# Walking the pairs of row tiles from the longest to the shortest in both attentions of a hybrid encoder

## The reference, cut to what matters

```python
def _fox_attend(q, k, v, c_q, c_k, pos_q, pos_k):          # forgetting attention, 4 heads
    s = jnp.einsum('bqhd,bkhd->bhqk', q, k) * HD_B ** -0.5
    s = s + (c_q[..., :, None] - c_k[..., None, :])        # sums of log forget values
    s = jnp.where(pos_k[None, :] <= pos_q[:, None], s, -jnp.inf)
    return softmax(s) @ v

def _dsa_attend(q, k, v, iq, ik, iw, cid_q, cid_k, k_top): # sparse attention, 4 heads, one K/V
    score = sum over 8 index heads of relu(iq . ik) * iw   # admissible keys only
    sel = top 256 keys of each row by score
    return softmax(q . k[sel]) @ v[sel]
```

## Time and profile before

| | |
|---|---|
| median of three runs | 2187.8 us (2182.45, 2187.8, 2193.98) |
| the profiled execution | 2186.85 us, its span 2185.2 us |
| mean granted clock of TensorE | 0.972 |
| busy: TensorE, VectorE, ScalarE, GpSimd | 1951.6, 1398.9, 734.6, 263.3 us |
| forget attention of layer 1, pairs and unit 8 | 692.4 to 846.8 us |
| sparse attention of layer 1 | 846.8 to about 966 us |
| forget attention of layer 2, pairs and unit 8 | 1776.0 to 1921.3 us |

### The profile page before, as it was taken

The page is one execution under the profiler, slowest core; times in us unless marked ns, Lnnn a source line. Parts: engine busy times, 40 slices in busy tenths (PEclk is TensorE's granted clock), DMA queues, the critical chain, the costliest instruction groups (busy, mean ns, idle before and its releaser), DMA issues. The chain is left out here.

```text
span 2185.2 us, 27310 instructions
## 1 busy us (share of the span) xinstructions
PE 1951.6 (89%) x9690; PEld 1091.6 (50%) x9690; DVE 1398.9 (64%) x2963; ACT 734.6 (34%) x1678; POOL 263.3 (12%) x362
## 2 busy tenths in 40 slices
PE   3999999989997777989969999999999977789997
PEld 2534456555444555654445344565554455556443
DVE  3268498889796773442232784989898968634422
ACT  2352134333112333543333522334331024344422
POOL 0000133232100000001100002233221000000011
PEclk9999999999998889999979999999999999999999
DMA  7201213121413002314351022221214130032242
GB/s 276 97 25 70 75 59 124 59 86 43 140 37 78 16 3 90 92 40 153 111 200 61 21 74 73 90 95 58 99 44 125 37 74 15 3 94 88 84 153 103
DMA packets 151272, 178.34 MB, mean 82 GB/s; under 512 B 71408, under 2 KB 106736, under 8 KB 150864
## 3 DMA queue, kind: packets, MB, share of 16 engines
q1 hardware_dynamic: 123072, 139.19, 20.3%
q10 hardware_dynamic: 28064, 37.38, 4.8%
HBM read 119.72 MB, written 66.69 MB: 85 GB/s over the span
## 5 line engine op out<-in xcount | busy, mean ns | idle before, releaser
L908 PE MATMUL ps<-wring,xnT_arena 128*128 128x512 f32 (+2 forms) x2304 | 920.6, 542 | 0.0
L908 PEld LDWEIGHTS ps<-wring,xnT_arena 128*128 128x128 f32 x2304 | 404.5, 192 | 354.0 <-issue 337.3
L1754 DVE TENSOR_SCALAR_CACHE_REDUCE arena<-arena,theta 32x1056 bf16<-32x1056 f32 x496 | 461.0, 979 | 2.3
L1391 ACT COPY arena<-ps 128x512 f32<-128x512 f32 (+3 forms) x144 | 75.4, 524 | 448.4 <-PE ps L908 414.8
L1269 PE MATMUL ps<-wring,xnT_arena 128*128 128x512 f32 x512 | 223.8, 595 | 0.0
L2028 DVE TENSOR_REDUCE mneg<-ps 128x1 f32<-128x192 f32 (+9 forms) x148 | 114.0, 770 | 120.7 <-PE ps L1201 118.6
L1269 PEld LDWEIGHTS ps<-wring,xnT_arena 128*128 128x128 f32 x512 | 96.4, 191 | 115.3 <-issue 115.3
L2196 POOL TENSOR_TENSOR arena<-arena 128x1024 f32<-128x1024 f32 (+1 forms) x16 | 35.4, 2215 | 757.9 <-DVE arena L1980 568.8
L1044 PEld LDWEIGHTS ps<-arena 128*128 128x128 f32 x488 | 69.6, 193 | 107.0 <-DVE arena L1861 78.5
L1044 PE MATMUL ps<-arena 128*128 128x128 f32 x488 | 80.4, 288 | 39.6 <-DVE arena L1861 39.4
L1199 PE MATMUL ps<-xnT_arena,arena 128*128 128x512 f32 (+4 forms) x240 | 97.1, 525 | 10.6 <-DVE xnT_arena L1356 9.1
(11 more groups left out here) (269 smaller groups left out, 2529.7 us busy)
## 6 DMA issues: line engine op xcount, KB each, us to landing
projected<-arena ACTq DMA_DIRECT2D x130, 256.0 KB, 2.0
arena<-residual SPq DMA_DIRECT2D x34, 512.0 KB, 5.1
wring<-in_w_in SPq DMA_DIRECT2D x16, 1024.0 KB, 7.8
o_bc<-projected SPq DMA_DIRECT2D x36, 384.0 KB, 3.7
wring<-in_w_in SPq DMA_DIRECT2D x6, 2048.0 KB, 8.8
wring<-in_w_out SPq DMA_DIRECT2D x8, 1024.0 KB, 6.4
residual<-arena SPq DMA_DIRECT2D x16, 512.0 KB, 2.7
out<-arena SPq DMA_DIRECT2D x16, 512.0 KB, 4.0
```

Of the source, the lines that this page charges most:

```text
L908: o = mm(bank(pbank(k), 0, w_), xnT[:, c, t * P:(t + 1) * P], w, start=(c == 0), stop=(c == CH - 1))
L1391: nc.scalar.copy(stage[s][:, 0:wide], bank(pbank(k), 0, wide)).then_inc(p_ev, 1)
L1754: V.tensor_scalar(cmp_out[0][r, (i % 2) * WMAX:(i % 2) * WMAX + uw[u]], score[u][r], th_, 0.0, op, ALU.add, accum_out=into[r, i:i + 1]).th ...
```

## The change

The four pairs are listed in the reverse order, in both attentions: (3, 7), (2, 6), (1, 5), (0, 4). The sample unit stays first and unit 8 last. All else follows from the list.

```diff
-        UNIT_GROUPS = [["s"]] + [[t, t + 4] for t in range(NT - 5)] + [[NT - 1]]
+        UNIT_GROUPS = [["s"]] + [[t, t + 4] for t in reversed(range(NT - 5))] + [[NT - 1]]
         AU = [(m, u) for m in ("fox", "dsa") for group in UNIT_GROUPS for u in group]
         AJ = [(m, u, h) for m in ("fox", "dsa") for group in UNIT_GROUPS for h in (range(H) if group != ["s"] else [0]) for u in group]
```

## The result

The changed kernel takes 2197.84 us (median of 17 runs, 2190.69 to 2201.89) against 2188.7 us for the kernel before on the same chips (17 runs, 2181.1 to 2201.64). The two medians lie 9.1 us apart; the ratio of the two sets of runs is 1.0031, 95% interval 1.0016 to 1.0047, which is 3.5 to 10.3 us slower with 6.8 in the middle, and inside the 0.5% that I had set as the bound of no difference. The forecast was 2194 us, with +7.2 us. So the sum was right; whether its terms were is another question. The profiled execution took 2200.29 us, its span 2198.6 at a mean granted clock of 0.971. That execution is 2.5 us above the median of its kernel.

What follows compares the result with a forecast made beforehand. VectorE was taken to bound all four forget pairs, TensorE the sparse attention. Per layer 1.6 + 3.0 - 1.0 = +3.6, twice, +7.2 us on 2186.85: forecast 2194 us, range 2172 to 2208.

Steps and rivals of the forecast that it cites:

- no difference: Whole kernel: a rival with 2187 to 2189 us, chance 0.12; differences within 0.5% (11 us) count as none.
- Start: Before the first forget pair: eight key tiles turned instead of five, five load buffers, first score 3.0 us later per layer.
- The pairs' order: Forget pairs: TensorE bounds the first, VectorE the others; 117.0 us against a mean of 115.4, +1.6 per layer.
- The three tiles: Inside the forget pairs: three key-tile turns disappear, worth between 0 and 5.3 us, taken as -1.0 per layer.
- Unit 8 of the forget attention: After the forget pairs: its work stays; between -6.3 in one layer and +6.3 in the other, taken as 0.
- The sparse attention: Sparse pairs: TensorE bounds, so order does not matter; 1.9 us of idle time may hide or show, taken as 0.
- The chances: Whole kernel: same within 0.5% 0.52, slower 0.30, faster 0.18.
- Slower by the clock: Rival, first pair and unit 8 of the forget attention: TensorE's clock drops, giving 2205 us; chance 0.30.
- Faster by stalls: Rival, forget attention: pair 0+4's turn-back never late, tiles worth 5.3 us, unit 8 31.32 us in both layers; 2173 us, chance 0.18.

Runs made afterwards that it cites:

- e4: The change itself run again, both attentions reversed, against the kernel before: 2195.8 us, ratio 1.0037.
- e1: Pairs reversed in the forget attention only, sparse attention in the old order, against the kernel before: 2190.02 us, ratio 1.0009.
- e2: Pairs reversed in the sparse attention only, forget attention in the old order, against the kernel before: 2193.89 us, ratio 1.0021.
- e11: The kernel before without its last two search rounds and with penalties set to zero, key tiles still inside the pairs: forget pairs 85.40 and 85.38 us.
- e7: The change without the last two search rounds and with penalties set to zero: 2136.26 us in one run.
- e6: Old order, key tiles 5 to 7 turned before the first pair, without the last two search rounds, penalties set to zero: 2129.27 us in one run.
- the bare kernel: The kernel before without its last two search rounds and with penalties set to zero (e11): forget pairs 85.40 and 85.38 us.
- e8: Old forget order with key tiles 5 to 7 turned before the first pair, sparse order 3+7, 0+4, 1+5, 2+6, 8: 2190.7 us against 2190.76 before.

## Why the prediction was right, and where only its sum was

*Start, +3.0 per layer.* Right in size, and half right in cause. The step that I had worked out, from the turn of queries to the first score in layer 2, took 6.92 us in e4 after 3.98, +2.94, and 7.52 in the first profile (1776.51 to 1784.03), +3.54, where its first turn of queries ran at the lower clock (1.09 us for four instructions, 0.63 in e4). Of my 3.0, 1.6 were loads behind a buffer and 1.4 turns; measured in e4 are 0.96 and 2.0. From maximum to maximum the start grew by 3.5 and 4.1 between the two profiles and by 3.4 in the means (8.3 us in the change, its repetition and e1, 4.9 in before, e2 and e11, with 4.3 to 6.3 among the latter): there the first scores are wider, which I had left out. The sixth buffer takes 0.5 to 1.4 us off it.

*The pairs' order, +1.6.* Right in size and, as far as e7 shows, wrong in cause. Measured +1.6, and +1.8 without any search or penalties beside the pairs (e7 against e6), where the balance on which I built it does not exist, and where 1.1 of it is work that the cut moves out of unit 8's stretch. How much of the +1.6 with the search in place is real cost, no run separates. My mean of 115.4 for the pairs of before was 0.3 too high, since the first window of the earlier trace rows starts at a score and not at a maximum; from it the same sum gives +1.9. The stretches by themselves came out near: forecast 33.0, 27.8, 25.1 and 31.1 us with the tiles' 1.0 to come off; measured 31.72, 26.10, 24.90 and 30.65. VectorE's busy times are those of my sum (24.6, 23.6, 20.9, 27.1 forecast; 24.10, 23.51, 20.92, 27.18 measured). TensorE's work in the first pair was not: 26.57 us at clock 1.00 in layer 2, where I had 30.9. I had moved pair 3+7 as a block, and its stretch held 203 matmuls; the new one holds 167 with the sample unit's 27 among them. The first scores of unit 8 had been in the old one. The first pair is still TensorE's, by 2.6 us (26.57 against 24.00) and not by 6.3.

*The three tiles, -1.0, with -5.3 as the bound.* Mis-sized. From the mean of before and e2 (116.1 us in four layers) to 111.3 it is -4.8, in before alone (115.1) -3.9, and -2.95 with no search. The step that failed is that I took the wait of 1.30 us for a rare one; in the bare kernel it comes in 1+5 and 2+6, in both layers. With the search in place the gain lies in the same two pairs, 27.9 to 24.9 us in 1+5 and 26.6 to 24.8 in 2+6 by the means. Why 1+5 gives 3 us there and 1.46 in the bare kernel stays open.

*Unit 8 of the forget attention, 0 with 6.3 either way.* Right on average: 33.8 us in the eight layers of the new order, 33.3 in the fourteen of the old one, with 32.0 to 36.6 in the one and 31.3 to 37.6 in the other. It holds some 20 matmuls fewer in the new order, so equal lengths are no proof that the order is free here. The 37.64 of layer 1 was that execution's, and not the layer's.

*The sparse attention, 0, bounds -1.9 and +1.9.* **This step failed.** I had written that TensorE bounds there, and that the sum of the pairs then does not depend on their order. At clock 1.00 throughout it goes from 109.6 to 112.0 us, +2.4, outside my bounds; over all profiles the mean is 113.3 (ten layers) against 110.8 (sixteen), and e2 puts +4.6 us on two layers. I had let the sample unit hide the idle time of the long pair, and the short pair show the same again. In the table by pairs, 3+7 does not hide but gains 0.8 us at the front, and 0+4 idles in any place. The idle time that came is 0.8 in 3+7, 0.6 in 1+5, 0.4 in 2+6 and 1.2 in unit 8, less 0.1 in 0+4: +2.8, with 0.45 us less of busy time; against e1's windows, which hold as many records as the new order's, it is +2.3 at equal busy time. So all of the growth is idle time. Its two largest parts stand on TensorE's timeline as single waits. The changed kernel, pair 3+7 and unit 8:

```profile
857.98 0.30 PE L1257 MATMUL ps<-cf,xnT_arena 128*128 128x128 f32 x1 [0.77 <-ACT arena L1582]
...
940.26 0.41 PE L1199 MATMUL ps<-arena 128*128 128x64 f32 x2 [1.16 <-DVE xnT_arena L1356]
```

and the kernel before, pair 0+4:

```profile
860.71 0.30 PE L1257 MATMUL ps<-cf,xnT_arena 128*128 128x128 f32 x1 [0.77 <-ACT arena L1582]
```

The first is a turn-back that waits for ScalarE's copy of a preparation, as in e11. It goes with the first place: before it stood in 0+4, in the change and in e8 it stands in 3+7, and 0+4 in last place has waits for VectorE in its stead (0.79, 0.57 and 0.77 us), so its idle time hardly falls. The second, in unit 8's window, waits for VectorE's copy of turned scores; it is 1.16 us behind 0+4, 0.36 behind 2+6 in e8, and not there behind 3+7. Nothing so plain shows in 1+5 and 2+6. My reading of the table is that TensorE fills the end of a pair with the first scores of the next, so what it can fill with depends on the neighbours; for unit 8 the waits fit that. For 3+7 they speak for the first place instead, and no run tells the two apart, since 3+7 stands first in both orders in which a smaller pair follows it. So that the old order is the better one is shown, and where most of the loss sits; this mechanism is only argued.

*Sum.* By the runs, per layer: start +3.4, tiles -3.9 to -4.8, order +1.6, unit 8 +0.5, sparse +2.5: +3.2 to +4.1 after a forecast of +3.6. These terms are means over profiles, and single ones swing by more than the sum. **The sum was right because two misses of about 3 us, the tiles and the sparse attention, cancelled.** The chances were fair for a result inside 0.5%, but the reasons behind them were in part not those that acted.

*The rivals.* Slower by the clock: its condition, unit 8 of layer 2 at or under 0.8 and the first pair under 1.00, held in e4 (0.77 and 0.95) and not in the first profile (0.87 and 1.00). It comes and goes between executions of one program, in either order. Two slices of 5 us in pair 0+4 of the changed kernel:

```profile
790.00:795.00 5.00, 2.08 (x18) 1.40 (x16) 4.93 (x7) 0.56 (x3) 0.00 (x0) 0.97 0.00 0
795.00:800.00 5.00, 2.47 (x20) 1.90 (x20) 3.10 (x7) 1.56 (x6) 0.00 (x0) 0.50 0.01 3
```

TensorE fell to 0.50, which is 1.2 GHz, behind a slice with 2.08 us of work, as in the earlier trace rows. The clock over the last pair was 0.81 and 0.89 where the last pair before had 0.90 and 0.91. That is the dip I feared, at a place where VectorE bounds, and it cost nothing that shows. Unit 8's first scores, on TensorE's timeline of the changed kernel, layer 1 and layer 2:

```profile
805.37 4.18 PE L1199 MATMUL ps<-xnT_arena,arena 128*128 128x64 f32 x6 [2.36 <-DVE xnT_arena L1356]
...
1892.56 2.18 PE L1199 MATMUL ps<-xnT_arena,arena 128*128 128x64 f32 x6 [1.56 <-DVE xnT_arena L1356]
```

The same work took 4.18 us in layer 1, where the clock from 805 to 810 us was 0.50, and 2.18 in layer 2, where it was 1.00 from 1892 to 1897 us. The Trainium skill, in TensorE: Matmul & The Clock Gate (What's actually happening), says that the throttled state is the default and that activity releases it. I had read from this, in the prediction, that by it alone unit 8 would start at 1.2 GHz each time. Here it did in one layer and not in the other, so the trace does not bear my reading out as a rule for this place. Faster by stalls: half of it came. The tiles were worth 3.9 to 4.8 of their 5.3, but in front of the scaled output in 0+4 VectorE still waited 2.44 us for the turn-back (timeline of VectorE in the changed kernel, layer 1):

```profile
800.64 0.28 DVE L1963 TENSOR_TENSOR o_bc<-ps,rinv 32x128 f32<-32x128 f32 x1 [2.44 <-PE ps L1257]
```

*What stays open.* The two profiled spans differ by 13.4 us, half as much again as the medians' 9.1. The windows of the attentions account for 6.4 of it; 7.3 lies between them, in stages that the change does not touch (815.3 us from the last maximum of layer 1 to the first of layer 2, then 822.6). That stretch is 822.6, 819.7 and 820.9 us in the three profiles with both attentions reversed and the search in place, 816.1 in the bare one, and 814.6 to 818.4 in the ten others. The profiled executions of the change and of e4 were 2.5 and 5.9 us above the medians of their kernels, so part of this is the choice of execution. No run here tells what the rest is.

## What to carry to other kernels

When a list's order is changed, ask first what else is derived from it: here the list also decided how many key tiles are turned in advance, and this by-product alone (old order, tiles first: ratio 0.9974) was the only part worth having. A stretch cut at a marker of one engine also holds work of the next stage that was issued ahead, so a block cannot be moved with its busy time; count its matmuls. And cost the quiet stage, too: a TensorE-bound pipeline with no other engine near its limit still paid 2.4 us a layer for the order of its blocks, while the terms of the stage that I had studied cancelled to about 1 us a layer (e1, with an interval that holds zero).

## What the runs showed that I had not expected

A preparation of 0.68 us of TensorE time cost 1.46 us inside a pair, since it pushed another one in front of a turn-back that shares its bank. In the first pair of the same kernel it cost nothing, and in the last pair, under VectorE's bound, one tile more or less cost nothing either: here its place in the list decided, not its work. The granted clock of one and the same stretch, unit 8 of the forget attention, was anything from 0.77 to 0.94 in executions of the same or nearly the same program, worth up to 6 us: a difference between two single profiles in such a stretch says nothing until it has been seen several times.
